# Strassen chunks of a streaming encoder on one core: T2 summed from stored weights by two accumulating DMAs, with a semaphore for each sum

## The reference, cut to what matters

```python
def conv_ffn(h, p, buf):
    u = h @ p['w_ffn_up']                    # (T, 1024) @ (1024, 2*2816)
    a, v = u[..., :D_FF], u[..., D_FF:]
    T = a.shape[1]
    ext = jnp.concatenate([buf.astype(a.dtype), a], axis=1)
    w = p['ffn_conv_w']
    c = p['ffn_conv_b'] + sum(ext[:, j:j + T] * w[j] for j in range(CONV_W))
    out = (jax.nn.silu(c) * v) @ p['w_ffn_down']   # (T, 2816) @ (2816, 1024)
    return out, ext[:, -(CONV_W - 1):]
```

## Time and profile before

| | |
|---|---|
| runs | 1936.17, 1929.79, 1938.61 us; median 1936.17 us |
| profiled execution | 1932.28 us; span 1930.5 us, mean granted clock 0.979 |
| PE busy | 1820.8 us (94% of the span), 11636 matmuls |
| DVE, ACT, POOL busy | 1267.4, 951.0, 229.5 us |
| DMA queue q1 (SP) | 144.39 MB, 23.5% of 16 engines' span |
| DMA queue q0 (POOL) | 39.86 MB, 12.6% of 16 engines' span |
| the two mixers with Strassen chunks | about 525 to 915 us and 1470 to 1860 us of the span |

### The profile page before, as it was taken

How to read it: one execution, slowest core, us unless ns; L and a number is a source line. 1 busy time by engine, 2 the same in 40 slices (tenths; PEclk the granted TensorE clock), 3 DMA queues, 4 the chain that set the end, 5 groups by cost and what they waited for, 6 DMA issues and landing times.

```text
span 1930.5 us, 31256 instructions
## 1 busy us (share of the span) xinstructions
PE 1820.8 (94%) x11636; PEld 1668.9 (86%) x11636; DVE 1267.4 (66%) x1973; ACT 951.0 (49%) x1593; POOL 229.5 (12%) x257
## 2 busy tenths in 40 slices
PE   8999999999899999898799999999998999999985
PEld 7999975698899999898799999657988999999984
DVE  5777875526765665677767778653377665756776
ACT  5444546436653443535654444653466343535355
POOL 0000034100112121111000000340001111111100
PEclk9999999999999999999999999999999999999997
DMA  4312131411565665565131122323125565556621
GB/s 178 91 57 68 62 95 52 134 54 40 130 159 142 153 142 141 138 156 140 44 106 46 57 68 72 88 74 96 60 76 145 142 151 143 141 149 166 140 71 60
DMA packets 98902, 204.03 MB, mean 106 GB/s; under 512 B 16864, under 2 KB 35680, under 8 KB 98728
## 3 DMA queue, kind: packets, MB, share of 16 engines
q1 hardware_dynamic: 63952, 144.39, 23.5%
q0 software_dynamic: 21888, 39.86, 12.6%
q10 hardware_dynamic: 12912, 17.78, 2.8%
HBM read 170.98 MB, written 8.65 MB: 93 GB/s over the span
## 4 chain that ended last, share of the span: by engine, by line
PE 56%; DVE 17%; DMA 13%; ACT 9%; issue 3%; DVEq 0%; POOL 0%; ACTq 0%; SPq 0%; POOLq 0%
PE G L795 34%; PE WA L795 11%; PE WB L795 8%; DVE wlo L2158 5%; DMA t<-in_wstream 4%; DMA wraw<-in_wstream 2%; ACT whi L1480 2%; DMA t<-wraw 2%; DVE tmp L2158 2%; DMA wff<-in_wstream 2%; DVE cc L2158 1%; DMA wraw<-t 1%; DMA wff<-t 1%; PE G L799 1%; DVE ax L2158 1%
## 5 line engine op out<-in xcount | busy, mean ns | idle before, releaser
L795 PE MATMUL G<-Hh,wlo 128*128 128x328 f32 x1384 | 452.4, 327 | 11.8 <-DVE Hl L2158 8.0
L795 PE MATMUL G<-Hh,whi 128*128 128x328 f32 x1384 | 436.0, 315 | 0.0
L795 PE MATMUL G<-Hl,whi 128*128 128x328 f32 x1384 | 434.6, 314 | 0.0
L795 PEld LDWEIGHTS G<-Hh,wlo 128*128 128x128 f32 x1384 | 263.2, 190 | 23.3 <-DVE Hl L2158 12.1
L795 PEld LDWEIGHTS G<-Hh,whi 128*128 128x128 f32 x1384 | 263.4, 190 | 2.4 <-issue 0.6
L795 PEld LDWEIGHTS G<-Hl,whi 128*128 128x128 f32 x1384 | 263.1, 190 | 0.0
L1480 ACT ACTIVATE whi<-wraw 128x1024 fp32r<-128x1024 f32 (+2 forms) x171 | 155.6, 910 | 187.0 <-PE G L795 114.7
L2158 DVE TENSOR_TENSOR wlo<-wraw,whi 128x1024 fp32r<-128x1024 f32 (+2 forms) x171 | 177.6, 1038 | 54.4 <-ACT whi L1480 41.8
L795 PE MATMUL G<-gh,wlo 128*128 128x328 f32 x424 | 134.3, 317 | 10.1 <-DVE tmp L2158 9.3
L795 PE MATMUL G<-Sh,wlo 128*128 128x328 f32 x304 | 100.9, 332 | 34.2 <-ACT R L1480 34.2
L795 PE MATMUL G<-gh,whi 128*128 128x328 f32 x424 | 132.9, 313 | 0.0
(11 more groups left out here) (327 smaller groups left out, 4142.9 us busy)
## 6 DMA issues: line engine op xcount, KB each, us to landing
wraw<-in_wstream SPq DMA_DIRECT2D x108, 512.0 KB, 3.5
wff<-in_wstream SPq DMA_DIRECT2D x40, 512.0 KB, 4.6
t<-in_wstream SPq DMA_DIRECT2D x76, 256.0 KB, 4.4
t<-in_wstream POOLq DMA_DIRECT2D x38, 256.0 KB, 6.5
ckT<-in_ckT SPq DMA_DIRECT2D x12, 512.0 KB, 3.4
wff<-in_wstream POOLq DMA_DIRECT2D x20, 256.0 KB, 4.1
t<-wff POOLq DMA_DIRECT2D x20, 256.0 KB, 3.9
wff<-t POOLq DMA_DIRECT2D x20, 256.0 KB, 3.5
```

What stands on the lines that cost most here:

```text
L795: return pe.matmul(out, lhsT, rhs, start=start, stop=stop, skip_group_check=True)
```

## The change

1. `summed`: the shared semaphore `T`, which counted T1, T2 and T4 in one sequence, becomes three, `T1`, `T2` and `T4`. A sum then waits for the sums that it needs and for its own predecessor. The names `lbd` and `y_raw` are merged into `conv` and `s_dve`, with their counts shifted.
2. T2 is made by two accumulating DMAs from HBM onto B22: first v, and, when that has landed, a. It no longer reads T1. `sum_t2(l, c, 1)` is the first of them, `sum_t2(l, c, 0)` the second. There are 38 Strassen chunks in the two layers, and so 38 more DMAs of 256 KB.
3. POOL's order. For the first Strassen chunk of a group: T1, T2 first part, T2 second part, T3. Then, within the group: T2 first part and T1 of chunk c+1, T4 of chunk c, T2 second part and T3 of chunk c+1.
4. The last piece of the layer's down product (`whi_x`, `wlo_x`) is split after the high and low parts of chunk 21's gated output (`gh`, `gl`), not before the SiLU of that chunk.
5. In the down product of group 0, DVE makes the low part of chunk 2's gated output (`g_low`) before the split of the last piece and the sums of activations (`Sf`), not behind them.

```diff
         def summed(l, c, i):
-            j = chunk_no(l, c)
-            return ("T3", 16 * (j + 1)) if i == T3 else ("T", 16 * (3 * j + {T1: 1, T2: 2, T4: 3}[i]))
+            return {T1: "T1", T2: "T2", T3: "T3", T4: "T4"}[i], (32 if i == T2 else 16) * (chunk_no(l, c) + 1)
...
                 if c > NPL:
-                    sum_wait(l, c - 1, T4)
+                    sum_wait(l, c - 1, T1)
                 pool.dma_start(v[:, 0:W_HALF], a["wstream"][l, S_UP[c // FH] + 2 * (c % FH)][:, 0:W_HALF],
-                               accum_op=ALU.add).then_inc(S("T"), 16)
-            def sum_t2(l, c):
-                j, v = chunk_no(l, c), raw_of(P_CHUNK[c] + 1)
-                pool.wait_ge(S(f"t2_in{j % 2}"), 16 * (j // 2 + 1))
-                sum_wait(l, c, T1)
-                pool.dma_start(t2[:, j % 2, :], v[:, 0:W_HALF], accum_op=ALU.add).then_inc(S("T"), 16)
+                               accum_op=ALU.add).then_inc(S("T1"), 16)
+            def sum_t2(l, c, first):
+                j, s = chunk_no(l, c), S_UP[c // FH] + 2 * (c % FH)
+                if first:
+                    pool.wait_ge(S(f"t2_in{j % 2}"), 16 * (j // 2 + 1))
+                    if c > NPL:
+                        sum_wait(l, c - 1, T2)
+                else:
+                    pool.wait_ge(S("T2"), 32 * j + 16)
+                pool.dma_start(t2[:, j % 2, :], a["wstream"][l, s + first][:, 0:W_HALF], accum_op=ALU.add)\
+                    .then_inc(S("T2"), 16)
...
                 pool.wait_ge(S("w_split"), unit_of(j, B21) + 1)
                 sum_wait(l, c, T2)
-                pool.dma_start(w[:, W_HALF:W_PIECE], t2[:, j % 2, :], accum_op=ALU.add).then_inc(S("T"), 16)
+                if c > NPL:
+                    sum_wait(l, c - 1, T4)
+                pool.dma_start(w[:, W_HALF:W_PIECE], t2[:, j % 2, :], accum_op=ALU.add).then_inc(S("T4"), 16)
...
-                sum_t1(l, NPL)
-                sum_t2(l, NPL)
                 for c in range(NPL, KF):
-                    sum_t3(l, c)
+                    if c in (NPL, GROUPS[group_of(c)][0]):
+                        sum_t1(l, c)
+                        sum_t2(l, c, 1)
+                        sum_t2(l, c, 0)
+                        sum_t3(l, c)
+                    within = c + 1 < GROUPS[group_of(c)][1]
+                    if within:
+                        sum_t2(l, c + 1, 1)
+                        sum_t1(l, c + 1)
                     sum_t4(l, c)
-                    if c + 1 < KF:
-                        sum_t1(l, c + 1)
-                        sum_t2(l, c + 1)
+                    if within:
+                        sum_t2(l, c + 1, 0)
+                        sum_t3(l, c + 1)
...
                     for v in split_after.get(e, ()):
+                        if v == UNITS_L - 1:
+                            continue
...
                     g_high(last_c)
+                    if q == NQ - 1:
+                        w_high(l, UNITS_L - 1)
...
                     else:
+                        g_low(last_c)
                         lows(l, u0 - 1)
...
-                    g_low(last_c)
+                    if q:
+                        g_low(last_c)
+                    if q == NQ - 1:
+                        w_low(l, UNITS_L - 1)
```

More of the change, by code:

```diff
@@ L1600, in _ @@
                             if not x and k == 5:
-                                act.wait_ge(S("lbd"), 1)
+                                act.wait_ge(S("conv"), 1)
                                 did(f(lbs[:, 1, 0, :], lbs[:, 0, 0, :], ACT.Exp, scale=-1.0), "lb_exp")
@@ L1919, in silu @@
                 def silu(c):
-                    act.wait_ge(S("conv"), l * KF + c + 1)
+                    act.wait_ge(S("conv"), 1 + l * KF + c + 1)
                     k, d = l * KF + c, tmp[:, c % 2, :]
@@ L2060, in scale_out @@
                 def scale_out(x, k):
-                    act.wait_ge(S("y_raw"), KD * x + k + 1)
+                    act.wait_ge(S("s_dve"), S_DVE * DEPTH + KD * x + k + 1)
                     did(f(Y[:, k, cols_of(x)], Y[:, k, cols_of(x)], ACT.Copy, scale=cols[:, 0, C_FIN + k:C_FIN + k + 1]),
@@ L2176, in _ @@
             dve.wait_ge(S("cols_in"), 16)
-            did(tt_(lbs[:, 0, 0, :], cols[:, 0, C_LB1:C_LB1 + HG], cols[:, 0, C_LB0:C_LB0 + HG], ALU.subtract), "lbd")
+            did(tt_(lbs[:, 0, 0, :], cols[:, 0, C_LB1:C_LB1 + HG], cols[:, 0, C_LB0:C_LB0 + HG], ALU.subtract), "conv")
             def add_square(n, k, first):
@@ L2915, in out_a @@
                 dve.wait_ge(S("rstd_end"), 1)
-                did(tt_(Y[:, k:k + 2, cols_of(0)], X[:, k:k + 2, cols_of(0)], spread(0, 2), ALU.mult), "y_raw", by=2)
+                did(tt_(Y[:, k:k + 2, cols_of(0)], X[:, k:k + 2, cols_of(0)], spread(0, 2), ALU.mult), "s_dve", by=2)
             scaled_b(KD - 3)
```

## The result

The changed kernel takes 1939.66 us (median of 20 runs, 1935.80 to 1949.21), the kernel before 1934.70 us beside it (20 runs, 1926.89 to 1940.25): ratio 1.0032, 95% interval 1.0020 to 1.0044. The forecast was 1923 us, in the range 1900 to 1943, with faster as the likeliest outcome. The profiled execution took 1937.62 us, span 1935.8 us, against 1932.28 and 1930.5 us.

A forecast was written before the change was run, and what follows sets the result against it. Prediction: PE, busy 94%, idles 40.3 us behind `R` and `p`, mostly for late T3. Chunks -9.5, group 0 +1.9, last group -2.7: -10.3 us from 1932.3 gives 1922.0, named 1923, range 1900 to 1943.

The forecast's parts named there:

- What bounds the kernel: Strassen chunks: PE idles 40.3 us behind `R` and `p`, mostly at third chunks, as T3 comes behind three successive sums.
- T3 is no longer late: Third chunks: T3 lands at about 618, ACT ready at 619.1, so PE's gap before product T2 goes.
- T3 stays last: Rival, chance 0.20: T3, fifth in the sums' queue with a single buffer, stays as late; only moved splits count, 1931.5 us.
- T4 becomes third in a queue: T4 of chunk c stands behind T2's first part and T1 of chunk c+1; third chunks' gap moves before product T1.
- First term, the landing: Three sums issued at once, T4 third: it lands after 7.4 us, 4.0 for one plus 1.7 for each further.
- Second term, the second chunks: Second chunks of groups: T4's delay hardly shows on PE, 0.2 us for each of 10.
- Third chunks: Eight third chunks keep gaps: 2.9 us before product T1 and 0.7 us for the late copy `p`, each.
- The clock: PE can stand at half clock after a gap; third chunks keep gaps of this size, so 0 counted.
- Group 0: +1.9 us: Down product of group 0: `gl` now ahead of DVE's `Sf` sums, 0.95 us later, twice; gap 4.9 to 5.9 us.
- Last group: -2.7 us: End of last group: moved split leaves the chain to `tmp`, 1.33 us, twice; gap 2.55 to 1.2 us.
- T4 later than T3 was: Rival, chance 0.18: three sums land at 9.0 us, total 1955 us; no gain from a landing of 7.9 us.
- T4 in time: Rival, chance 0.12: three sums overlap and land at 4.0 us; all 40.3 us of gaps go, total 1881.6 us.

The follow-up runs named there:

- e5: Kernel before with only a semaphore for each sum, T2 still made from T1, order and splits as before: 1892.19 us, ratio 0.9783.
- e4: Kernel before with only chunk 2's `g_low` moved ahead of the sums `Sf` in group 0's down product: 1934.74 us, ratio 1.0003.
- e3: Kernel before with only the split of the layer's last down piece moved behind chunk 21's high and low parts: 1928.63 us, ratio 0.9966.
- e13: T3 issued ahead of T2's second part, against a kernel with separate semaphores and T2 from stored weights (1926.28 us): 1941.46 us, ratio 1.0040.
- e1: Changed kernel with T4 of chunk c issued ahead of T2's first part and T1 of chunk c+1: 1907.69 us, ratio 0.9854.
- e6: Changed kernel with T4 of chunk c issued second, between T2's first part and T1 of chunk c+1: 1909.51 us, ratio 0.9879.

## Why the prediction was wrong

- **In short.** The step that failed is T4's landing against the moment when PE needs it. The prediction had the third sum of a burst land after 7.4 us, and took the second chunks to hardly notice it (0.2 us each). It landed after 7.9 us, and the second chunks have 21.5 us of waits where 2.0 were forecast.
- **What bounds the kernel: right.** T3 late behind three sums in a row, read from the earlier trace rows. `e5` removes one wait in that chain and gains 42.8 us. But I priced the chain's removal only together with the rest of the change. The row that shows this wait was at hand: T1 of chunk 8 "2.94 <-DMA wff<-t".
- **T3 is no longer late: right.** No split of T2 and T3 waits for a DMA after; the rival "T3 stays last" falls.
- **T4 becomes third in a queue: right in place, wrong in size. First term, the landing, "4.0 + 2 x 1.7 = 7.4 us".** At the 28 places where T4 is third, it lands 6.99 to 9.12 us after the first's issue, median 7.85 (7.94 at the 24 where the three go out within 1.2 us), and 7.9 was what I had given as the point of no gain. By the prediction's own 20 us for each us, these 0.45 us are an estimated 9 of the 15 us by which the time is off (-10.3 forecast, +5.0 measured).
- **Second term, the second chunks: "I count 0.2 us for each of the 10".** Their waits are 21.5 us, 2.1 us each, and their time over 12.64 us rose from 1.4 to 34.2 us. I had argued from 0.63 us of idle on ACT. In the trace after, T4 of chunk 7 lands at 619.86, 1.8 us before product T1 is due (621.6), and ACT and PE need 3.1 us from the landing to that product; it starts 1.3 us late, the gap of 1.13 us. The prediction's own figures left no room: T4's split at 614.5 and 3.2 us more give 617.7, and PE came for product T1 of chunk 7 just then, before:

```profile
617.68 0.31 PE L795 MATMUL G<-Sh,wlo 128*128 128x328 f32 x1
```

  Set beside that frame (chunk 7 starts 3.96 us later after), the burst started 0.5 us later than forecast and took 1.1 us longer. And I left out the second gap: the copy `p` follows late, which I had counted at third chunks (0.7 us) and not here (1.05 us).
- **Third chunks: "8 x (2.9 + 0.7)", 28.8 us.** Measured are 21.7 us of waits, 7.1 less. The gap moved from before T2 to before T1, as forecast. That a part of the delay is now waited off in the second chunk already would explain the smaller figure; no run tests it.
- **In one measure:** 30.8 us of waits behind `R` and `p` were forecast, there are 44.3. The 13.5 us between them are +19.5 in the second chunks, -7.1 in the third and +0.9 in the fourth. They are nearly all of the 14.2 us between the forecast of the chunks, -9.5 us, and the +4.7 us by which the two stretches of chunks grew in the profile (-1.9 and +6.7).
- **The clock: "I count 0".** Right in total: the time over 12.64 us that is not a wait was 20.8 us and is 22.1 us.
- **The fourth chunks and chunks 3 and 5** lost 15.7 us of the time over 12.64 us (11.8 to 0.9 us of waits), as the forecast had it: their waits were in the 40.3 us that it took off. With the 11.9 us that the third chunks lost, it nearly made up for the second.
- **Group 0: +1.9 us.** The gap grew as worked out, from 4.92 to 5.86 us, in PE's timeline after:

```profile
524.98 0.64 PE L808 MATMUL WB<-gh,wlo 128*128 128x328 f32 x1 [5.86 <-ACT Y L1493]
```

  `e4` has it in its trace too, but its time can't tell 1.9 us from nothing.
- **Last group: -2.7 us.** The gap behind `tmp` after is as forecast (waits of PE at 915 to 935 us), the timed gain of `e3` is larger, 3.9 to 9.1 us:

```profile
PE G L808 <- DVE tmp L2175: 1.2, 1, 1.2
```

- **The rivals.** "T4 later than T3 was" had the mechanism, the point from which it decides and the sign; its price was for landings of 9.0 us, which only the latest reached. "T4 in time", which the Trainium skill's page "DMA: Bandwidth & Descriptors", section "Anatomy of one DMA", would give by its fixed cost and bandwidth, does not occur: three sums need 7.9 us, twice its estimated 3.8 us.

## What to carry to other kernels

One semaphore for several chains makes every later DMA wait for the latest of them: look for such a shared counter first, and change it alone, since here that one edit gave 2.2%, and the rewrite that came with it turned the gain into a loss of 0.3%. Where DMAs are issued together, put the one whose consumer is due next first; a place further back costs 1.9 to 2.6 us of landing here. A new form that trades a dependence for a second DMA is judged by the whole loop from one chunk's last sum to the next one's, in the order of issue, not by the link it removes, and if two operands are split by one instruction, it waits for the later of them, and making one earlier at the other's cost gains nothing (`e13`).

## What was not expected of the hardware

- Sums by accumulating DMAs queue almost one behind the other: T4 of 256 KB lands after 3.4 us as the first of a burst, 6.0 us as the second and 7.9 us as the third, counted from the burst's first issue (medians of 28; `e1`, `e6` and the change). Queue q0's share of the 16 engines follows their number:

```profile
q0 software_dynamic: 27360, 49.82, 15.7%
```

  That is 3.1 points of the span for 9.96 MB more than before [12.6%, 39.86 MB], 6.1 us of all engines per MB, against 3.1 us per MB for SP's plain loads on q1 (23.5% for 144.39 MB).
